# A two-layer decoder trunk on one core: softmaxes of two head halves put between the products of the projections

## The reference, cut to what matters

```
h = rms_norm(x, norm_mix);  q, k, v = (h @ w_in) as 3 x 16 heads of 64
heads 0-3:   q, k as 8 groups of 32: rms_norm, rotary on 8 columns; p = softmax(q1 k1) - lam * softmax(q2 k2)
             o = rms_norm(p v, subln) * (1 - lam_init)
heads 4-9:   q, k rms_norm over 64, rotary on 16 columns; mixture of three dilated windows
             (one softmax with the logs of counts added as a mask)
heads 10-15: the same q, k; causal softmax
x = x + concat(o) @ w_out
x = x + memory_cross_attention(rms_norm(x), rms_norm(mem) @ w_mkv) @ w_mo
x = x + (silu(g) * u) @ w_down,   g, u = rms_norm(x) @ w_gate_up
```

## Time and profile before

| what | us |
|---|---|
| median of 3 runs | 829.86 (828.04 to 837.52) |
| the profiled execution | 833.84 |
| its span | 832.0 |
| PE busy | 749.0 (90%) |
| DVE busy | 525.5 (63%) |
| ACT busy | 350.2 (42%) |
| POOL busy | 190.8 (23%) |
| mean granted clock | 0.922 |

### The profile page before, as it was taken

How to read it: one execution, slowest core, us unless ns; L and a number is a source line. 1 busy time by engine, 2 the same in 40 slices (tenths; PEclk the granted TensorE clock), 3 DMA queues, 4 the chain that set the end, 5 groups by cost and what they waited for, 6 DMA issues and landing times.

```text
span 832.0 us, 11776 instructions
## 1 busy us (share of the span) xinstructions
PE 749.0 (90%) x4476; PEld 658.6 (79%) x4476; DVE 525.5 (63%) x890; ACT 350.2 (42%) x488; POOL 190.8 (23%) x107
## 2 busy tenths in 40 slices
PE   5989679988699999999989967899888999999997
PEld 4877458867589999999878755688677999999996
DVE  5699653577765656466566985555666566556553
ACT  5754354425423433343346525435344434343331
POOL 5058520352420000000231782106324000000000
PEclk9999758998899999999999987599868999999999
DMA  8844520043336557765477443101513457765651
GB/s 310 335 152 152 184 95 1 20 133 102 101 108 196 151 161 218 205 173 151 159 251 256 143 151 128 52 1 51 152 52 103 150 153 210 204 188 151 179 174 50
DMA packets 122654, 122.83 MB, mean 148 GB/s; under 512 B 2944, under 2 KB 95232, under 8 KB 122624
## 3 DMA queue, kind: packets, MB, share of 16 engines
q1 hardware_dynamic: 119744, 113.26, 44.8%
q0 software_dynamic: 2160, 7.87, 2.7%
q10 hardware_dynamic: 720, 1.32, 0.5%
HBM read 121.38 MB, written 1.05 MB: 147 GB/s over the span
## 4 chain that ended last, share of the span: by engine, by line
PE 65%; DVE 25%; ACT 4%; issue 2%; DMA 2%; POOL 1%; ACTq 0%; DVEq 0%; POOLq 0%
PE ps L1451 29%; PE ps L1153 8%; PE ps L1466 5%; PE ps L1467 5%; PE ps L1468 5%; DVE wlo L716 4%; PE ps L1223 3%; DVE ny L728 2%; DVE nt L727 2%; DVE lam_z L921 2%; PE ps L1239 2%; PE ps L1402 1%; DVE sq L911 1%; DVE xn L744 1%; DVE nv L731 1%
## 5 line engine op out<-in xcount | busy, mean ns | idle before, releaser
L716 DVE TENSOR_TENSOR wlo<-raw,whi 128x2048 fp32r<-128x2048 f32 x80 | 190.5, 2403 | 35.3 <-ACT whi L491 35.1
L491 ACT ACTIVATE whi<-raw 128x2048 fp32r<-128x2048 f32 (+1 forms) x108 | 200.1, 1873 | 28.9 <-PE ps L1153 15.8
L418 POOL TENSOR_TENSOR wlo<-raw,whi 128x2048 fp32r<-128x2048 f32 (+1 forms) x28 | 122.6, 4388 | 371.0 <-ACT whi L491 370.9
L680 ACT ACTIVATE qkv<-qkv 128x256 f32<-128x256 f32 x44 | 18.4, 418 | 236.3 <-DVE qkv L1062 236.3
L1451 PE MATMUL ps<-thi,whi 128*128 128x256 f32 x704 | 102.3, 289 | 1.4 <-ACT thi L496 1.4
L1451 PE MATMUL ps<-thi,wlo 128*128 128x256 f32 x704 | 101.4, 288 | 0.0
L1451 PEld LDWEIGHTS ps<-thi,whi 128*128 128x128 f32 x704 | 96.1, 197 | 5.3 <-ACT thi L496 2.0
L1451 PE MATMUL ps<-tlo,whi 128*128 128x256 f32 x704 | 98.9, 283 | 0.0
L1451 PEld LDWEIGHTS ps<-thi,wlo 128*128 128x128 f32 x704 | 93.7, 198 | 0.0
L1451 PEld LDWEIGHTS ps<-tlo,whi 128*128 128x128 f32 x704 | 91.1, 192 | 0.0
L1062 DVE TENSOR_TENSOR qkv<-ps,qkv 128x256 f32<-128x256 f32 x44 | 18.7, 424 | 95.9 <-PE ps L1451 95.9
(11 more groups left out here) (168 smaller groups left out, 963.4 us busy)
## 6 DMA issues: line engine op xcount, KB each, us to landing
raw<-in_w_gate_up SPq DMA_DIRECT2D x88, 512.0 KB, 5.4
raw<-in_w_in SPq DMA_DIRECT2D x24, 1024.0 KB, 5.2
raw<-in_w_down SPq DMA_DIRECT2D x22, 1024.0 KB, 5.0
raw<-in_w_out SPq DMA_DIRECT2D x8, 1024.0 KB, 5.2
raw<-in_w_mkv SPq DMA_DIRECT2D x4, 1024.0 KB, 5.5
xn<-in_mem POOLq DMA_DIRECT2D x2, 1024.0 KB, 6.2
raw<-in_w_mq SPq DMA_DIRECT2D x4, 512.0 KB, 3.4
raw<-in_w_mo SPq DMA_DIRECT2D x2, 1024.0 KB, 5.0
```

The source lines that it names most:

```text
L418: pool.tensor_tensor(wlo[s][:, 0:n], raw[s][:, 0:n], whi[s][:, 0:n].bitcast(F32), ALU.subtract)\
L491: act.activation(whi[s][:, 0:n], raw[s][:, 0:n], ACT.Copy).then_inc(hi_done[s].sem, 1)
L716: dve.tensor_tensor(wlo[s][:], raw[s][:], whi[s][:].bitcast(F32), ALU.subtract)\
```

## The change

The work is cut into two halves of heads (0 to 7 and 8 to 15), and the chunks come in the order of `COLUMNS`: q, k, v of the first half, q, k, v of the second. PE's main sequence becomes a list of 96 fillers: filler g is four products (one K half, one token tile, one of the three passes). Fillers 0 to 71 are the six chunks, 72 to 83 the memory's projection, 84 to 95 the first half of w_out, which uses heads 0 to 7 only. Every other step stands at a filler number, from tables at the end of the file, on all engines: PE issues the steps of g ahead of filler g, and ACT and DVE go through the same g with their own order within one.

Chunk tiles take three banks in turn. Transposed probabilities, and q and k of the second half, share bank 2 (`take_bank2`: each waits until the last user's copy is done). The gain of the rotated columns is multiplied into cos and sin tables (40 columns instead of 12), the gain of the other columns, q's and k's in one, is a scale per partition when k is copied out after its transposes. The first half of w_out is added to x ahead of the second (`add_out0`). The transposed heads go to `hhi`, `hlo`, which lie over `qT`, `kT`. The memory is transposed in four quarters at g 72 and 73. POOL splits units 8 to 17. The diff, cut to its core:

```diff
+COLUMNS = (0, 2, 4, 1, 3, 5)
-ROT = ((2 * DIFF, 32, 4, 0, 0), (DIL + MOBA, 64, 8, DIFF * HD, 4))
+ROT = (((2 * DIFF, 32, 4, 0, 0), (4, 64, 8, 4 * HD, 8)),
+       ((2, 64, 8, 8 * HD, 8), (6, 64, 8, 10 * HD, 24)))
+NROT = 40
...
+                def rope_q(half):
+                    pool.wait_ge(scaled.sem, scaled.at(layer, 2 * half + 1))
+                    for n, rot in enumerate(ROT[half]):
+                        v, cos, sin, m, lo, hi = rotary(0, rot, rope)
+                        pool.tensor_tensor(m[0], v, cos, ALU.mult)
+                        link(pool.tensor_tensor(m[1], v, sin, ALU.mult))
+                        pool.tensor_tensor(v[:, :, :, lo], m[0][:, :, :, lo], m[1][:, :, :, hi], ALU.subtract)
+                        ins = pool.tensor_tensor(v[:, :, :, hi], m[0][:, :, :, hi], m[1][:, :, :, lo], ALU.add)
+                        if n:
+                            ins.then_inc(roped.sem, 1)
+                        else:
+                            link(ins)
...
+                for u in range(DVE_LO, U_MQ):
+                    if u == ROPE_BEFORE:
+                        rope_q(1)
                     split_lo(layer, u)
...
-                def chunk_out(c):
-                    act.wait_ge(used[(2 * c + 1) % RING].sem, used_after(layer, 2 * c + 1))
-                    if c == 0:
+                def chunk_out(i, t):
+                    if t == 0:
+                        act.wait_ge(tile_done.sem, tile_done.at(layer, i + 1))
+                    else:
+                        act.wait_ge(used[(2 * i + 1) % RING].sem, used_after(layer, 2 * i + 1))
+                    if i == t == 0:
                         act.wait_ge(rs_ready.sem, rs_ready.at(layer, 1))
+                    c = COLUMNS[i]
+                    act.activation(qkv[:, t, 512 * c:512 * c + 512], ps[:, proj_bank(i, t), :], ACT.Copy,
+                                   scale=rs[:, 0, t:t + 1]).then_inc(proj_out.sem, 1)
+                def square(e):
+                    i = QK_CHUNKS[e]
+                    act.wait_ge(proj_out.sem, proj_out.at(layer, T * (i + 1)))
+                    if e:
+                        act.wait_ge(scaled.sem, scaled.at(layer, e))
+                    act.activation(sqc[:], heads_of_half(e % 2, e // 2), ACT.Square).then_inc(sqr.sem, 1)
...
+                for g in range(6, LAST + 1):
+                    for i in range(NCHUNK):
+                        for t in range(T):
+                            if g == 12 * i + 9 + 3 * t:
+                                chunk_out(i, t)
                     for t in range(T):
-                        ins = act.activation(qkv[:, t, 512 * c:512 * c + 512], ps[:, 4 + 2 * (c % 2) + t, :],
-                                             ACT.Copy, scale=rs[:, 0, t:t + 1])
-                    ins.then_inc(proj_out.sem, 1)
-                for c in range(NCHUNK - 1):
-                    split_hi(layer, 2 * c + 3)
-                    if layer == 0 and c == 0:
+                        if g == 12 * NCHUNK + 9 + 3 * t:
+                            mkv_tile(t)
+                    for q in range(4):
+                        if g == MEM_AT[q]:
+                            x_hi(layer, X_MEM, q)
+                    for m in range(0, HEADS, 2):
+                        if g == T_AT[m]:
+                            probT_out(m)
+                    for e, i in enumerate(QK_CHUNKS):
+                        if g == 12 * i + 12:
+                            square(e)
...
+                    if g % 6 == 0 and g // 6 + 2 < U_MQ:
+                        split_hi(layer, g // 6 + 2)
+                    if layer == 0 and g == 6:
 
                         act.wait_ge(mem_in.sem, 16)
...
+                def scale_qk(e):
+                    part, half = e % 2, e // 2
+                    dve.wait_ge(sqr.sem, sqr.at(layer, e + 1))
+                    if half == 0:
+                        link(dve.tensor_reduce(g32[:, :, 0:16], sqc[:].rearrange("p t (g w) -> p t g w", w=32), AX_X, ALU.add))
+                        v = nv[:, 0:T * 12].rearrange("p (t g) -> p t g", t=T)
...
+                    w = 4 if half == 0 else 8
+                    dve.tensor_tensor(z, z, r.unsqueeze(3).to_broadcast((P, T, w, HD)), ALU.mult)\
+                       .then_inc(scaled.sem, 1)
+                    if part == 0:
+                        return
+                    dve.wait_ge(s_tab.sem, s_tab.at(layer, 1))
+                    dve.wait_ge(scaled.sem, scaled.at(layer, e + 1))
+                    for n, rot in enumerate(ROT[half]):
+                        v, cos, sin, m, lo, hi = rotary(1, rot, rope_dve)
+                        dve.tensor_tensor(m[0], v, cos, ALU.mult)
+                        link(dve.tensor_tensor(m[1], v, sin, ALU.mult))
+                        dve.tensor_tensor(v[:, :, :, lo], m[0][:, :, :, lo], m[1][:, :, :, hi], ALU.subtract)
+                        ins = dve.tensor_tensor(v[:, :, :, hi], m[0][:, :, :, hi], m[1][:, :, :, lo], ALU.add)
+                        if n:
+                            ins.then_inc(roped_dve.sem, 1)
+                        else:
+                            link(ins)
...
+                for g in range(6, LAST + 1):
+                    for q in range(4):
+                        if g == MEM_AT[q]:
+                            x_lo(layer, X_MEM, q)
+                    for m in range(1, HEADS, 2):
+                        if g == T_AT[m]:
+                            probT_out(m)
+                    for d in range(DUOS):
+                        if g == S_AT[d]:
+                            mask_max(2 * d)
+                            mask_max(2 * d + 1)
+                        if d < DIFF and g == S_AT[d] + 4:
+                            combine(d)
+                    for e in range(4):
+                        if g == QKT_AT[e]:
+                            qkT_out(e)
+                        if g == 12 * QK_CHUNKS[e] + 13:
+                            scale_qk(e)
+                    if layer == 0 and g == 14:
+                        lambdas()
+                        dve.wait_ge(s_memss.sem, 1)
+                        mean_eps(nv[:, 0:T], mem_ss[:], D)
+                        rsqrt(T)
+                        dve.tensor_copy(mem_r[:], ny[:, 0:T]).then_inc(s_memr.sem, 1)
+                    if g == V_AT[7] + 1:
                         heads_out(0).then_inc(o_read.sem, 1)
-                    if d in MEM_AT:
-                        half_lo(layer, B_MEM, MEM_AT.index(d))
+                        sub_norm()
...
+                    if g % 6 == 1 and g // 6 + 2 < DVE_LO:
+                        split_lo(layer, g // 6 + 2)
+                    for n in range(4):
+                        if g == 12 * (NCHUNK + 1) + 3 * n + 3:
+                            add_out0(n // 2, n % 2)
+                    if g == KM_AT:
+                        mem_keys()
+                heads_out(1).then_inc(heads_ready.sem, 1)
+                heads_lo(2)
+                heads_lo(3)
...
+                def proj_piece(i, h, t, part):
+                    if h == part == 0 and T * i + t >= 3:
+                        pe.wait_ge(proj_out.sem, proj_out.at(layer, T * i + t - 2))
+                    ins = piece(2 * i + h, t, part, proj_bank(i, t), 4 * h, h == 0, h == 1,
+                                split=(t_hi, t_lo, 4 * X_MIX + 2 * t + h + 1) if i == 0 else None)
...
+                def filler(g):
+                    c, p = divmod(g, 12)
+                    (h, t), part = divmod(p // 3, 2), p % 3
+                    if c == 0 and layer:
+                        h, t = t, h
+                    if c < NCHUNK:
+                        proj_piece(c, h, t, part)
+                    elif c == NCHUNK:
+                        mkv_piece(h, t, part)
+                    else:
+                        out0_piece(h, t, part)
+                bank2 = []
+                def take_bank2(sig, n):
+                    if bank2:
+                        before, m = bank2.pop()
+                        pe.wait_ge(before.sem, before.at(layer, m))
+                    bank2.append((sig, n))
+                def transpose_qk(e):
+                    if e % 2 == 0:
+                        pe.wait_ge(roped.sem, roped.at(layer, e // 2 + 1))
+                    else:
+                        pe.wait_ge(roped_dve.sem, roped_dve.at(layer, e // 2 + 1))
+                    part, half = e % 2, e // 2
+                    for b in range(2):
+                        if e == 1:
+                            if b == 0:
+                                pe.wait_ge(qkT_act.sem, qkT_act.at(layer, 1))
+                            else:
+                                pe.wait_ge(qkT_dve.sem, qkT_dve.at(layer, 1))
+                        if e >= 2:
+                            take_bank2((qkT_act, qkT_dve)[b], e + 1)
+                        for j in range(2):
+                            for t in range(T):
+                                a = j * SEQ + t * P
```

(72 more changed lines are left out.)

659 lines of the change are left out of this document (293 added, 366 removed).

## The result

The changed kernel takes 861.2 us (median of 4 runs, 859.12 to 862.78), beside 828.95 for the kernel before in the same session: a ratio of 1.037, with an interval of 1.032 to 1.041. The forecast was 816 and a gain; it was wrong in its sign and 45 us off. The profiled execution has a span of 860.7 us (832.0 before). Among one kernel's times there are sometimes two groups some 4 to 8 us apart, so differences under 4 us are not read.

A forecast was written before the change was run, and what follows sets the result against it. PE should bound but waits: 41.1 us of layer 1's 174.6 were waits and low clock. With 131.8 work and 29.1 waits, layer 1 gains 12.0, layer 0 1.6; 829.9 - 13.6 = 816 us, range 788 to 838.

The forecast's parts named there:

- g 35 to 37: K of half 0: POOL's gain of mem holds a small DVE instruction; wait of 4.5 us, between 0 and 5.7.
- g 51: Transposes of q's second half: PE waits 7.3 us for POOL's rotation and 0.7 for ACT's copy, 8.0 in all.
- g 61 to 68: K of half 1: DVE's scaling and rotation, held by POOL's split of unit 12, delay PE; taken as 6.0 us.
- g 70 to 73: Shared bank 2 costs 1.0 us, memory's first product waits 0.9 for hi and lo; 1.9 in all.
- g 82 to 84: Heads' norm on DVE before masks 14 and 15 costs 0.5 us, heads_hi(1) behind ACT's copy 0.9; 1.4 in all.
- g 86 to 92: Memory keys' norm on DVE before masks 18 and 19, beside POOL's split 16; taken as 2.5 us, between 0 and 3.7.
- End: End of the window: heads_out(1) and last hi and lo exposed, 2.5 us, x for the cross stage 0.5; 3.0 in all.
- Work: PE's products, scores, probability steps and transposes in one layer's window sum to 131.8 us at full clock.
- the copy behind mem's squares: Layer 0: ACT squares mem before copying the first tile, so the fourth tile waits; 5.0 us, between 1.3 and 6.6.
- Behind g 51 that costs 1.8: Low PE clock after the idle time before q's second transposes, 1.8 us in layer 1; it can't be below 0.
- Rival 3: Waits at g 35, 51 and 68 keep PE's clock low, one 24 us stretch a layer; 840 us, chance 0.15.
- a clock of 0.5 for over 10 us: Sign that the forecast is wrong: granted PE clock of 0.5 for over 10 us in a layer's heads.

The follow-up runs named there:

- number 6: Changed kernel with POOL waiting, before its gain of mem and its splits 12 and 16, until DVE's chains there are through; 848.3 us, ratio 1.019.
- number 7: Changed kernel with unused dummy products on PE, 46 ahead of filler 51 and 28 each ahead of 67, 80 and 90; 851.3 us, ratio 1.022.
- number 8: Changed kernel with q's second transposes at g 59, head 3's at 61, norms at 80 and 91, and POOL's three waits; 833.3 us, ratio 1.002.
- mended order: Number 9: on top of number 8, DVE's split of unit 7 behind its copy of k, q's first transposes at g 27; 820.1 us, ratio 0.990.
- exps late: Changed kernel with ACT's exponentials of duos 7 and 9 two fillers later, behind its copy of probabilities; 854.6 us, ratio 1.027.

## Why the prediction was wrong

**The terms, in the prediction's own order.** *g 35 to 37*: forecast 4.5, measured 2.71 + 2.21 = 4.9, by the collision named. *g 51*: 8.0, measured 7.24 + 0.69 = 7.9. *g 61 to 68*: 6.0, measured 4.9 (4.71, 0.22). *g 70 to 73*: 1.9, measured 1.5. These four were right in place and releaser, and within 1.1 us in size. *g 82 to 84*: 1.4, measured 4.58 + 1.75 = 6.3: I set the norm against the masks behind it and didn't follow the masks to ACT's exponential, the split and the copy queued behind that, and the bank that it frees. *g 86 to 92*: 2.5, measured 4.6, through the same chain; what made it long was the collision that the prediction named there, for with POOL's split held back it was 0.45 (number 6). *q's first half* in layer 1: 0, measured 2.67; POOL's two products of its rotation took 2.37 and 2.50 us instead of 0.45, beside DVE. *End*: 3.0, measured 2.5. Idle in all 35.4 against 27.3. In layer 0 the copy behind mem's squares was forecast at 5.0 and cost 1.58, and q's transposes 3.5 and 3.40. *Work*: 136.0 against 131.8, 4.2 too little. The rotation of q's first half in layer 1, POOL and then DVE:

```profile
461.26 2.37 POOL L471 TENSOR_TENSOR rope_pool<-qkv,tab 128x128 f32<-128x128 f32 x1 [12.52 <-DVE qkv L912]
463.60 2.50 POOL L472 TENSOR_TENSOR rope_pool<-qkv,tab 128x128 f32<-128x128 f32 x1
```

```profile
461.04 4.75 DVE L771 TENSOR_TENSOR wlo<-raw,whi 128x2048 fp32r<-128x2048 f32 x2
```

**The step that failed is the clock.** The prediction says "Behind g 51 that costs 1.8", and counts no other low clock but 1.7 at the start. Layer 0 had 2.2 and 1.8 in the same way. Measured are 15.5 us in layer 1 and 14.9 in layer 0: 23 of the 45 us of the miss, and more than the forecast gain of 13.6, so this term alone turns it into a loss. The rest is, in the main, idle time, 8.1 too little in layer 1 and 2.9 in layer 0, and work, 4.2 in each. Behind the wait of 7.24 us alone PE, busy 6.7 of 7.4 us, ran at 0.64; behind it the clock came back:

```profile
506.40:513.60 7.20, 0.00 (x0) 0.00 (x0) 3.53 (x14) 0.06 (x1) 2.94 (x9) 0.66 0.01 2
513.60:521.00 7.40, 6.69 (x25) 5.43 (x26) 2.29 (x6) 1.56 (x6) 4.45 (x1) 0.64 0.24 40
521.00:530.00 9.00, 9.00 (x56) 7.19 (x55) 2.74 (x13) 6.36 (x13) 4.61 (x1) 1.00 0.37 115
```

That is 2.4 us, near the 1.8. The error was to count it once. Behind the waits of 2.67, 2.21, 4.71, 4.58 and 4.60 us PE ran 3 to 5 us at 0.50 as well (behind the one of 4.58, 572.6 to 579.0 at 0.66), which cost 1.4 to 2.2 us each, and at the end, behind 1.70 and 0.83, over 6 us, which cost 3.0. With 1.7 at the start these are the 15.5. The forecast had such waits in its own list, without a price. The length of a wait alone doesn't tell the price: behind the one of 2.71 (482.62) and the one of 1.75 (584.16) the clock was 1.00. The Trainium skill, "TensorE: Matmul & The Clock Gate", names the gate; the price per wait comes from these rows.

**Under it lies a ledger not made.** I took 41.1 us of layer 1 as "waits and low clock" in one sum, beside 1.7 of low clock at the start, and set 29.1 against it. Measured, with the 1.7, are 39.7 where I had 42.8: the 3.1 between are work that the kernel before had too (134.9, not 131.8). Split, the 39.7 read 22.4 of idle and 17.3 of low clock, and my own forecast of idle, 27.3, is more than the kernel before had. So the gain of 12.0 was 13.8 of clock and 3.1 of work counted too low, less 4.9 of added idle: what was to be won came from the clock, on no argument but that slices would be dense. The kernel before loses 10.5 of its 17.3 in one thin stretch, the changed one its 15.5 in many short ones:

```profile
512.00:539.00 27.00, 21.05 (x89) 15.96 (x88) 13.80 (x48) 13.19 (x39) 4.52 (x1) 0.50 0.22 78
```

**Rival 3** (the clock stays low, slower, 840) had the right sign and engine, with a chance of 0.15, but in one stretch of 24 us; it was many short ones, and idle on top. "Idle under 20 us a layer", "no wait at g 51" and "a clock of 0.5 for over 10 us" were named as what would make the forecast wrong. Only the third came, spread out. Most of what was to show it right came as well: 7.24 us at g 51 released by POOL, the held instructions of DVE, no wait for the memory keys, a clock of 0.85 and 0.91 in the first two stretches shown at number 7. The signs on the waits tested the part that was right; only the one on the clock told of the failure.

**What the runs show of the cause.** The change's idea holds: with the same products and slices, another order gives 820. The 41 us between are the place of q's second transposes (17 us alone), POOL's instructions beside DVE's chains (13 alone), and the order of DVE's splits and q's first transposes (13 from number 8 to 9 by the medians, 11 by the lowest times; the two weren't tried apart). The place of head 3's transposes is in number 8 only and wasn't tried alone. Not a cause in the mended order: the place of the norms. The low clock comes with the waits: filling the four longest with useless work won 10 us. It doesn't follow the idle time in all: 15.5 was lost at idle 35.4, 7.5 at 24.6 and 6.5 at 19.6, but 17.3 at 29.3 (exps late) and 17.3 at 22.4 in the kernel before. What decides which wait costs how much stays open, and so does what made the work term 4.2 us larger than counted.

## What to carry to other kernels

Before a gain is forecast from a gap, split the gap into idle and low clock over the same window: a change that swaps one thin stretch for many waits can keep the clock's loss; here most waits of 2 to 7 us cost another 1.4 to 2.4 us behind them. Follow an inserted step through the in-order queue behind it until PE is reached, across engines and shared banks. Try the place of each slice alone before the scheme is judged: one number here was worth 17 us.

## What was not expected of the hardware

- Beside two POOL splits in a row one DVE instruction of 128x256 took 10.05 us instead of under 0.5. The Trainium skill, "SBUF — State Buffer", section "Who interferes with whom", tells of the lock for the length of one instruction; here it lasted through two (9.01 us).
- The hold goes the other way too: POOL's products of 128x128 took 2.37 and 2.50 us beside a DVE split, 0.45 without.
- 130 idle-filling products a layer made the changed kernel 10 us faster; 74 a layer made the mended one slower, by 4 to 7 us.
